# Two transformer stacks in one kernel: every joint between sites in a new order of input chunks, updates and weight splits

## The chip, the cores and the metric

The kernel runs on one core of a Trainium2 chip. The metric is the device time of one execution in microseconds, lower is better. TensorE multiplies 128x128 blocks into eight PSUM banks (`B[0]` to `B[7]`), VectorE (DVE), ScalarE (ACT) and GpSimd (POOL) work on tiles, SyncE (SP) issues most loads. Each engine runs its own instructions in order; semaphores tie them together.

## What is computed

The first block is two layers of latent attention, convolution, Fourier and gating branches on 256 tokens of width 1024. The second block, where the change sits, is twice this, for `x` of 256 x 1024:

```
h = rmsnorm(x, g[0]); x = x + 0.5 * rmsnorm(swiglu(h, w_gate0, w_up0, w_down0), g[1])
h = rmsnorm(x, g[2]); x = x + rmsnorm(token_mixer(h, w_in, w_out, ...), g[3])
h = rmsnorm(x, g[4]); x = x + 0.5 * rmsnorm(swiglu(h, w_gate1, w_up1, w_down1), g[5])
swiglu(h, g, u, d) = (silu(h @ g) * (h @ u)) @ d          # inner width 2816
rmsnorm(x, g) = x * rsqrt(mean(x * x) + 1e-6) * g
```

All in fp32 precision: each product is made of three products of a high and a low part.

## The kernel before

**Sites.** The second block is six sites (`SITES`): feed-forward 0, mixer 0, feed-forward 1, feed-forward 2, mixer 1, feed-forward 3. This text calls the stretch before site i joint i: joint 0 follows the first block, joints 1 and 4 lead from a feed-forward site into a mixer, joints 2 and 5 from a mixer into a feed-forward site, joint 3 from feed-forward 1 into feed-forward 2.

**Weights.** SyncE fills a ring of three 1 MB slots (`fill`, L525; `ffn`, L548). A slot holds two units of 128 x 1024. In a feed-forward site the slots come as gate, up, down; the units as gate half 0, up half 0, gate half 1, up half 1, down, and so on: unit 5 is the first of the second gate slot. For every unit ScalarE copies a high part (`high`, L987) and VectorE subtracts it to get the low part (`low`, L1570). There are six places for split units (`SPLIT`), so a high part waits until TensorE has used the unit six before (`s_used`). A slot is filled again when the low part of its last unit is done (`s_low`), so the second gate load of a site waits for the third unit's low part. `EARLY = 4`: up to four units of the next site are split ahead.

**A joint.** Each engine does `site_tail(i)` and then `site_norm(i + 1)`.
- The sums y of the site stand in banks 4 to 7, one per (token tile t, half hf of 512 columns). ScalarE squares each (L1051), takes the mean's parts (L1054) and the root (L1057).
- VectorE multiplies y by the gain (`gained`, L1634), takes the reciprocal (L1639) and updates the residual `X` with two passes of 512 columns a tile (`update`, L1644). Its order: gain both halves and update for tile 0, then the same for tile 1.
- TensorE warms up with a few products into bank 0 (`warm`, L2438) and transposes the eight 128-column chunks of each tile (`turned`, L2447): chunks 0 to 3 of tile 0, a warming product of 512, chunks 4 to 7 of tile 0, then all eight of tile 1.
- ScalarE copies each turned chunk (L1032) as the high input, VectorE makes the low input (`site_norm`, L1608). Chunks 6 and 7 share banks with 4 and 5 and wait for their low inputs.
- TensorE runs `first_units` (L2467): for each chunk four products of high inputs with high and low weights of two units (L2474, L2475), then two per chunk with low inputs (L2479).
- For the norm, ScalarE squares `X` (`x_square`, L994), VectorE sums and makes a diagonal (`inverse`, L1612), TensorE spreads it over the partitions (`norm_sum`, L2459) and ScalarE copies the row (`norm_row`, L1041). In a feed-forward site `norm_sum` stands after chunk 3 of the third unit, in a mixer right after `first_units`.
- The mixer's first results are scaled by that row when evicted (`evicted`, L1744). In a feed-forward site the row scales the gate (`gate_scaled`, L1658), then ScalarE's Silu (L1066), the product (`multiplied`, L1670), ScalarE's `hidden_high` (L1072) and VectorE's `hidden_low` (L1679), which the first down product waits for (`down`, L2519).

**The last down rows** of a feed-forward site (L2556 to L2564) run the first of three units over all four (t, hf), and then, for each (t, hf), the other two. VectorE and ScalarE split the last two down units and three units of the next site behind and between the last hidden parts (L1108 to L1119, L1725 to L1739), and the fourth in `site_norm`.

**Joint 0.** The last results of the first block are scaled into `ytmp` and added to the residual (`out_scaled`, L1271), the additions of three of the four (t, hf) on GpSimd (L671; those in `ADDED` on VectorE). Then squares (L1008), a root (L1016) and `final_scaled` (L1575), one tile after the other, with low parts of units 0, 2 and 1 between.

## Time and profile before

| | |
|---|---|
| median of 3 runs | 1435.17 us (1432.9 to 1436.27) |
| profiled execution | 1436.06 us |
| its span | 1434.1 us |
| TensorE busy | 1398.1 us |
| VectorE busy | 1018.7 us |
| ScalarE busy | 726.7 us |
| GpSimd busy | 86.7 us |

The profile is one execution, times in microseconds from the span's start. The execution's own time is the span and about 2 us around it. A busy TensorE can be a TensorE that warms up or runs at half clock, so joints are read from the order of instructions.

### The profile page before, as it was taken

To read this page: it belongs to the slowest core of one execution; us is meant where nothing else is said; L and a number is where in the kernel's file an instruction comes from. 1 tells how busy PE (TensorE), PEld (TensorE's weight loads), DVE (VectorE), ACT (ScalarE), POOL (GpSimd) and SP (SyncE) were. 2 spreads that over 40 slices of the span, in tenths; PEclk is the share of its full clock that TensorE was granted. 3 is DMA by queue.
4 is the path that set the end of the run, shared out by engine and by line. 5 is a ranking of instruction groups with operands and counts; after the bars stand their busy time and mean duration, and the time that the engine had idled before them with its cause. 6 is when DMAs were issued, how large, how long until landed. Compare 5 with 4: busy or idle time off the path is not lost.

```text
span 1434.1 us, 22170 instructions
## 1 busy us (share of the span) xinstructions
PE 1398.1 (97%) x8053; PEld 1159.8 (81%) x8053; DVE 1018.7 (71%) x1693; ACT 726.7 (51%) x1244; POOL 86.7 (6%) x103
## 2 busy tenths in 40 slices
PE   5999999999999999999999999999999999999998
PEld 2778747869768888888888888888888888888887
DVE  2588454469677777787686777877777876877776
ACT  3433264345565444475664444654445756644444
POOL 0301211220110000000200000000000002000000
PEclk9999999999999999999999999999999999999999
DMA  9622184275235655754345556646655643455662
GB/s 354 195 88 89 59 285 175 88 221 150 88 133 170 198 189 175 248 176 146 118 133 176 175 193 193 211 153 202 197 183 177 195 142 118 133 176 178 202 196 98
DMA packets 185654, 243.03 MB, mean 169 GB/s; under 512 B 4560, under 2 KB 154608, under 8 KB 185456
## 3 DMA queue, kind: packets, MB, share of 16 engines
q1 hardware_dynamic: 182272, 229.43, 49.9%
q0 software_dynamic: 2736, 10.55, 2.2%
q10 hardware_dynamic: 576, 2.10, 0.4%
q8 instruction: 46, 0.75, 0.2%
q14 instruction: 24, 0.20, 0.0%
HBM read 241.01 MB, written 1.05 MB: 169 GB/s over the span
## 4 chain that ended last, share of the span: by engine, by line
PE 69%; DVE 12%; DMA 9%; ACT 5%; issue 4%; POOL 0%; SPq 0%; DVEq 0%; ACTq 0%; POOLq 0%
PE bank L1977 33%; PE bank L2496 13%; PE bank L2498 7%; DMA weight_ring<-in_w_ffn_up 5%; DVE weights_low L1573 3%; ACT weights_high L992 3%; DVE arena L1567 2%; PE bank L2104 2%; DMA weight_ring<-in_w_ada 2%; DMA weight_ring<-in_w_ffn_down 2%; PE bank L1958 1%; DMA weight_ring<-in_w_in 1%; PE bank L2324 1%; PE bank L2474 1%; PE bank L2475 1%
## 5 line engine op out<-in xcount | busy, mean ns | idle before, releaser
L1573 DVE TENSOR_TENSOR weights_low<-weight_ring,weights_high 128x1024 fp32r<-128x1024 f32 x328 | 393.3, 1223 | 128.8 <-ACT weights_high L992 128.7
L992 ACT ACTIVATE weights_high<-weight_ring 128x1024 fp32r<-128x1024 f32 x328 | 334.6, 1048 | 102.1 <-PE bank L1977 62.0
L2496 PE MATMUL bank<-input_split,weights_high 128*128 128x512 f32 x1280 | 319.5, 391 | 0.0
L2496 PEld LDWEIGHTS bank<-input_split,weights_high 128*128 128x128 f32 x1280 | 234.7, 188 | 45.0
L2498 PEld LDWEIGHTS bank<-input_split,weights_low 128*128 128x128 f32 x1280 | 174.6, 190 | 12.5
L2498 PE MATMUL bank<-input_split,weights_low 128*128 128x256 f32 x1280 | 178.5, 282 | 0.0
L1977 PE MATMUL bank<-weights_high,hidden_high 128*128 128x512 f32 x352 | 138.8, 394 | 1.2 <-DVE hidden_low L1682 1.2
L1066 ACT ACTIVATE silu_gate<-gate_sum 128x256 f32<-128x256 f32 x88 | 36.7, 418 | 202.0 <-DVE gate_sum L1660 200.5
L1977 PE MATMUL bank<-weights_low,hidden_high 128*128 128x512 f32 x352 | 137.9, 392 | 0.0
L1977 PE MATMUL bank<-weights_high,hidden_low 128*128 128x512 f32 x352 | 137.0, 389 | 0.0
L1977 PE MATMUL bank<-input_split,weights_high 128*128 128x256 f32 x576 | 105.6, 285 | 0.0
L1072 ACT ACTIVATE hidden_high<-hidden 128x256 fp32r<-128x256 f32 x88 | 36.8, 418 | 129.8 <-DVE hidden L1673 123.7
L1977 PE MATMUL bank<-weights_high,input_split 128*128 128x256 f32 (+1 forms) x384 | 90.2, 323 | 0.5 <-issue 0.5
L1977 PEld LDWEIGHTS bank<-input_split,weights_high 128*128 128x128 f32 x576 | 89.5, 192 | 1.1 <-DVE qk_feature_major L1756 0.7
L1977 PE MATMUL bank<-hT_high,first_high 128*128 128x512 f32 (+1 forms) x248 | 89.6, 361 | 0.2 <-DVE weight_ring_low L1253 0.2
L1977 PE MATMUL bank<-hT_high,weight_ring_low 128*128 128x512 f32 (+1 forms) x248 | 86.9, 350 | 0.0
L1977 PE MATMUL bank<-input_split,weights_low 128*128 128x256 f32 x288 | 81.4, 283 | 0.0
L1977 PEld LDWEIGHTS bank<-weights_high,hidden_high 128*128 128x128 f32 x352 | 66.4, 189 | 14.3 <-issue 2.8
L1977 PEld LDWEIGHTS bank<-weights_high,hidden_low 128*128 128x128 f32 x352 | 66.1, 188 | 14.5
L1977 PEld LDWEIGHTS bank<-weights_low,hidden_high 128*128 128x128 f32 x352 | 66.4, 189 | 10.7
L1977 PEld LDWEIGHTS bank<-weights_high,input_split 128*128 128x128 f32 x384 | 64.4, 190 | 8.6 <-issue 3.5
L1682 DVE TENSOR_TENSOR hidden_low<-hidden,hidden_high 128x256 fp32r<-128x256 f32 x88 | 37.4, 425 | 43.7 <-ACT hidden_high L1072 43.7
(358 smaller groups left out, 2267.5 us busy)
## 6 DMA issues: line engine op xcount, KB each, us to landing
weight_ring<-in_w_ffn_gate SPq DMA_DIRECT2D x44, 1024.0 KB, 5.3
weight_ring<-in_w_ffn_up SPq DMA_DIRECT2D x44, 1024.0 KB, 5.3
weight_ring<-in_w_ffn_down SPq DMA_DIRECT2D x44, 1024.0 KB, 4.9
weight_ring<-in_w_in SPq DMA_DIRECT2D x32, 1024.0 KB, 5.3
weight_ring<-in_w_ada SPq DMA_DIRECT2D x24, 1024.0 KB, 6.0
weight_ring<-in_w_out SPq DMA_DIRECT2D x16, 1024.0 KB, 5.0
weight_ring<-in_w_in SPq DMA_DIRECT2D x24, 512.0 KB, 4.8
gain_row<-in_norm_gains POOLq DMA_DIRECT2D x6, 512.0 KB, 4.1
```

The lines of the kernel that those rows point to most:

```text
L992: A(unit_in(WH, U), unit_source(U), ACT.Copy).then_inc(s_high, 1)
L1066: A(sgate[:, par, :], gsum[:, par, :], ACT.Silu).then_inc(s_silu, 1)
L1072: A(HBH[:, par if to is None else to, :], hbuf[:, par, :], ACT.Copy).then_inc(s_hh, 1)
L1567: STT(accv, src, w, accv, ALU.mult, ALU.add).then_inc(*done("conv_tap", L, j, k))
L1573: TTn(unit_in(WL, U), unit_source(U), unit_in(WH, U).bitcast(F32), ALU.subtract).then_inc(s_low, 1)
L1682: TTn(HBL[:, to, :], hbuf[:, par, :], HBH[:, to, :].bitcast(F32), ALU.subtract).then_inc(s_hl, 1)
L1958: last = mm(b[32 * k:32 * k + 32, :], CS[:, 4 * q + k, :], quarters(n)[:, k, :], start=(q == 0), stop=(q == 1), skip_group_check=True)
L1977: last = mm(o, lhs(x), rhs(y), start=start and m == 0, stop=stop and m == 2, skip_group_check=True)
L2104: last = mm(b[out_rows, 0:ncol], lhs(k), hT[:, k, 0:ncol], start=(k == 0), stop=(k == KD - 1))
L2324: mm(b[:, 0:keys], Q[0:QK, h, seg * T + qt * P:seg * T + (qt + 1) * P], K[0:QK, h, k0:k0 + keys], start=True, stop=True).then_inc(*done("s ...
L2496: mm(b[:, :].rearrange("p (h n) -> p h n", h=2), unit_in(WH, U)[:, k, :], HX[:, k, :, :], start=(k == 0), stop=False, skip_group_check=True)
L2498: last = mm(b[:, 0:T], unit_in(WL, U)[:, k, :], HH[:, k, :], start=False, stop=(k == KD - 1), skip_group_check=True)
```

## The change

What it does, in all engines' queues:
- **Transposes.** Before `first_units` only chunks 0 to 3 of both tiles are turned, with a warming product of 256 between. The other eight transposes run inside `first_units`, behind chunk 2 of the high inputs.
- **Updates.** Tile 1's first 512 columns are updated in two pieces of 256, and its second gain pass stands behind them. `final_scaled` in joint 0 goes by pieces too: tile 0 first half, tile 1 two pieces, then both second halves.
- **Squares.** ScalarE takes the squares of `X` at other places; that of one (t, hf) per joint moves to VectorE (`tensor_tensor_reduce`), but not in joints 2 and 5.
- **Splits.** Behind a feed-forward site, units 2 and 3 of the next site get their high parts in the tail, behind each tile's root, and their low parts behind input chunk 5 and at the end of `inverse`. The last down unit is split before the last hidden parts. In joint 0 the low parts of units 1 and 3 stand behind chunks 3 and 5.
- **Head of a feed-forward site.** High parts of units 4 and 5 stand before the norm row's copy; the low part of unit 4 stands before the first gate sum, that of unit 5 before `hidden_low`. The norm sum moves from before chunk 3 to before chunk 5 of the third unit, in mixers from before that unit to before its chunk 4. Feed-forward 0 starts with units 0 and 2, both gates, then units 1 and 3, with the norm sum before chunk 2 of unit 3.
- **Last down rows.** Tile 0: units one and two, both halves, then unit three; tile 1: all three for half 0, then for half 1.
- **Joint 0.** All additions but one go to VectorE; ScalarE's table load stands behind two high parts.
- Some marks get other names.

The diff, cut to its core:

```diff
-ADDED = [{(0, 1), (1, 1)}, {(1, 1)}]
+ADDED = [{(0, 1), (1, 1)}, {(0, 1), (1, 0), (1, 1)}]
@@ ScalarE
-            A(stat[:, 60:61], eps[:, 0:1], ACT.Sqrt)
             act.wait_ge(*at("attn", 1, 0, 1))
             for unit in (0, 2):
                 high(unit)
+            A(stat[:, 60:61], eps[:, 0:1], ACT.Sqrt)
...
             def site_norm(i):
+                after_ffn = i and SITES[i - 1][0] == "ffn"
+                if i and not after_ffn:
                     x_square(i, 0, 0)
-                    x_square(i, 0, 1)
-                if i and SITES[i - 1][0] == "ffn":
-                    high(unit_base[i] + EARLY - 1)
                 for c in range(KD):
+                    if c == 4:
+                        x_square(i, 1, 0) if i else high(3)
...
-                for hf in range(2):
-                    x_square(i, 1, hf)
+                if not after_ffn:
+                    x_square(i, 0, 1)
+                if i == 0:
+                    x_square(i, 1, 0)
+                x_square(i, 1, 1)
+                if SITES[i][0] == "ffn":
+                    high(unit_base[i] + 4)
                 act.wait_ge(*at("x_mean", "ready", i))
                 A(stat[:, 8:10], stat[:, 6:8], ACT.Sqrt).then_inc(...)
-                high(unit_base[i] + 4)
                 if SITES[i][0] == "ffn":
                     A(stat[:, 60:61], eps[:, 0:1], ACT.Silu)
+                    high(unit_base[i] + 5)
+                else:
+                    high(unit_base[i] + 4)
                 act.wait_ge(*at("norm_sum", i))
                 A(norm_row, B[4][:, 0:T], ACT.Copy).then_inc(*done("norm_row", i))
-                high(unit_base[i] + 5)
+                if SITES[i][0] == "mix":
+                    high(unit_base[i] + 5)
@@ ScalarE, site_tail; the high part stands behind each root
+                            if t and i < 5 and SITES[i][0] == "ffn":
+                                x_square(i + 1, 0, 0)
...
+                    if i < 5 and SITES[i][0] == "ffn":
+                        high(unit_base[i + 1] + EARLY - 2 + t)
@@ ScalarE, end of ffn
                 high(a + 5)
+                high(a + 6)
                 hidden_high(1, f + 2, None, to=2)
-                high(a + 6)
-                for U in ahead[1:]:
+                for U in ahead[1:2]:
                     high(U)
@@ VectorE, site_norm, and the end of inverse
+                    if i == 0 and c == 3:
+                        low(1)
+                    if i == 0 and c == 5:
+                        low(3)
+                    if i and c == 5 and SITES[i - 1][0] == "ffn":
+                        low(unit_base[i] + EARLY - 2)
...
+                if i and SITES[i - 1][0] == "ffn":
+                    low(unit_base[i] + EARLY - 1)
@@ VectorE, site_tail
+                gained(0, 0)
+                gained(0, 1)
+                scale(0)
+                update(0, 0, slice(0, 512))
+                update(0, 1, slice(512, 1024))
+                gained(1, 0)
+                if i == 5:
+                    gained(1, 1)
+                    scale(1)
+                    update(1, 0, slice(0, 512))
+                else:
+                    if SITES[i][0] == "ffn":
+                        dve.wait_ge(*at("x_new", i, 0, 1))
+                        dve.tensor_tensor_reduce(out=XN2[:, 0, 512:1024], in0=X[:, 0, 512:1024], in1=X[:, 0, 512:1024], ...)
+                    scale(1)
+                    update(1, 0, slice(0, 256), "first")
+                    update(1, 0, slice(256, 512))
+                    gained(1, 1)
+                update(1, 1, slice(512, 1024))
@@ VectorE, head of ffn
                 inverse(i)
+                low(a + 4)
                 gate_parts(0, a + 1)
-                up_parts(0, a + 2)
-                low(a + 4)
                 dve.wait_ge(*at("norm_row", i))
                 gate_scaled(0, f0 + 1)
+                up_parts(0, a + 2 if n else 3)
+                multiplied(0, f0 + 1)
                 low(a + 5)
-                multiplied(0, f0 + 1)
                 hidden_low(0, f0 + 1)
@@ TensorE, site_norm
                 turned(0, (0, 1, 2, 3))
-                warm(1)
-                turned(0, (4, 5, 6, 7))
-                turned(1, (0, 1, 2, 3, 4, 6, 5, 7))
+                warm(1, 256)
+                turned(1, (0, 1, 2, 3))
+                return lambda: (turned(0, (4, 6)), turned(1, (4, 6)), turned(0, (5, 7)), turned(1, (5, 7)))
@@ TensorE, first_units
+                step_to = 1 if i else 2
...
+                    if c == 2:
+                        rest_turned()
@@ TensorE, end of ffn
-                down(1, a + 4, f, False)
-                for t in range(2):
-                    for hf in range(2):
-                        for par in range(2):
-...
+                lasts = ((1, a + 4, f), (0, a + 5, f + 1), (2, a + 6, f + 2))
+                for rest in (lasts[:2], lasts[2:]):
+                    for hf in range(2):
+                        for par, U, ready in rest:
+...
+                            down_row(par, U, 0, False, U == a + 6, (hf,))
+                for hf in range(2):
+                    for par, U, ready in lasts:
+                        last = down_row(par, U, 1, False, U == a + 6, (hf,))
```

## Rows read from the trace of the kernel before

**Rows 1.** The page, costliest groups: the two splitting helpers.

```profile
L1573 DVE TENSOR_TENSOR weights_low<-weight_ring,weights_high 128x1024 fp32r<-128x1024 f32 x328 | 393.3, 1223 | 128.8 <-ACT weights_high L992 128.7
...
L992 ACT ACTIVATE weights_high<-weight_ring 128x1024 fp32r<-128x1024 f32 x328 | 334.6, 1048 | 102.1 <-PE bank L1977 62.0
```

**Rows 2.** Windows: length; busy us of PE, PEld, DVE, ACT, POOL; clock; DMA; GB/s.

```profile
417.00:438.50 21.50, 18.95 (x109) 15.65 (x108) 18.08 (x33) 16.72 (x38) 3.10 (x3) 0.92 0.50 172
...
611.30:624.10 12.80, 10.60 (x72) 8.36 (x71) 11.18 (x32) 10.40 (x29) 0.53 (x1) 1.00 0.39 127
...
927.30:943.20 15.90, 15.69 (x105) 13.44 (x103) 14.07 (x30) 13.79 (x30) 0.53 (x1) 1.00 0.47 151
...
1240.70:1256.10 15.40, 15.40 (x105) 13.42 (x104) 13.03 (x28) 13.19 (x29) 0.59 (x1) 1.00 0.26 86
...
422.20:424.20 2.00, 0.00 (x0) 0.00 (x0) 1.91 (x4) 1.86 (x4) 0.00 (x0) 1.00 0.00 0
...
425.70:427.80 2.10, 2.10 (x11) 2.10 (x10) 1.88 (x5) 1.47 (x5) 0.04 (x1) 0.50 1.07 379
...
943.00:1091.00 148.00, 148.00 (x784) 127.64 (x783) 108.55 (x144) 65.91 (x89) 0.00 (x0) 1.00 0.60 192
```

**Rows 3.** Timeline of joint 3, VectorE: start, duration, instruction, idle before.

```profile
928.07 1.28 DVE L1634 TENSOR_TENSOR x_scaled<-bank,gain_row 128x512 f32<-128x512 f32 x2
...
929.46 1.41 DVE L1644 SCALAR_TENSOR_TENSOR residual<-x_scaled,stat,residual 128x512 f32<-128x512 f32 x2
...
942.55 0.43 DVE L1682 TENSOR_TENSOR hidden_low<-hidden,hidden_high 128x256 fp32r<-128x256 f32 x1 [0.89 <-ACT hidden_high L1072]
```

**Rows 4.** Timeline of joint 3, ScalarE.

```profile
928.22 0.29 ACT L1057 ACTIVATE stat<-stat 128x1 f32<-128x1 f32 x1
...
930.63 2.30 ACT L1032 ACTIVATE input_split<-bank,vectors_T 128x256 fp32r<-128x256 f32 x6
...
938.75 0.37 ACT L1041 ACTIVATE scaled_out<-bank 128x256 f32<-128x256 f32 x1
```

**Rows 5.** Timeline of joint 3, TensorE.

```profile
930.27 1.32 PE L2447 MATMUL bank<-const_base,residual 128*128 128x128 f32 x8 [0.21 <-DVE residual L1644]
...
931.34 0.36 PE L2474 MATMUL bank<-input_split,weights_high 128*128 128x256 f32 x1
...
935.26 2.08 PE L2479 MATMUL bank<-input_split,weights_high 128*128 128x256 f32 x16
...
943.23 0.47 PE L1977 MATMUL bank<-weights_high,hidden_high 128*128 128x512 f32 x1
```

**Rows 6.** Timeline of SyncE in joint 3, and the gate loads' time to landing.

```profile
924.74 0.38 SPq L564 DMA_DIRECT2D weight_ring<-in_w_ffn_gate  x1
...
DMA to landing us min/median/max: 5.2/5.3/6.6
```

**Rows 7.** Timeline of joint 1, ScalarE, TensorE and VectorE.

```profile
607.90 1.06 ACT L992 ACTIVATE weights_high<-weight_ring 128x1024 fp32r<-128x1024 f32 x1 [1.97 <-DMA weight_ring<-in_w_in]
...
613.68 0.64 PE L2447 MATMUL bank<-const_base,residual 128*128 128x128 f32 x4 [1.38 <-DVE residual L1644]
...
624.86 0.76 DVE L1756 SCALAR_TENSOR_TENSOR qk_feature_major<-bank,scaled_out 128x256 f32<-128x256 f32 x2 [1.28 <-ACT scaled_out L1041]
...
630.19 0.42 DVE L1756 SCALAR_TENSOR_TENSOR qk_feature_major<-bank,scaled_out 128x256 f32<-128x256 f32 x1 [0.60 <-PE bank L1977]
```

**Rows 8.** Timeline of joint 0, ScalarE, VectorE and TensorE.

```profile
412.44 2.00 ACT L992 ACTIVATE weights_high<-weight_ring 128x1024 fp32r<-128x1024 f32 x2
...
418.69 2.04 DVE L1582 SCALAR_TENSOR_TENSOR residual<-residual,stat,gain_row 128x512 f32<-128x512 f32 x2
...
424.26 1.82 PE L2447 MATMUL bank<-const_base,residual 128*128 128x128 f32 x8 [2.07 <-DVE residual L1582]
```

**Rows 9.** Timeline behind joint 4, VectorE's evictions in the second mixer.

```profile
1126.32 0.76 DVE L1756 SCALAR_TENSOR_TENSOR qk_feature_major<-bank,scaled_out 128x256 f32<-128x256 f32 x2 [1.28 <-ACT scaled_out L1041]
...
1131.65 0.42 DVE L1756 SCALAR_TENSOR_TENSOR qk_feature_major<-bank,scaled_out 128x256 f32<-128x256 f32 x1 [0.85 <-PE bank L1977]
```

More of the change, by code:

```diff
@@ L1538, in layer @@
                 if L:
-                    for b in range(2):
-                        third_branch_low(b)
+                    third_branch_low(0)
+                    third_branch_low(1)
+                    low(0)
+                    out_scaled(1, 0, 0)
+                    low(2)
+                    out_scaled(1, 0, 1)
+                    out_scaled(1, 1, 0)
+                    out_scaled(1, 1, 1)
+                    return
                 for t in range(nt):
@@ L1614, in inverse @@
                     for hf in range(2):
-                        dve.wait_ge(*at("sum_squares", "site", i, t, hf))
+                        if (t, hf) == ((0, 1) if i else (0, 0)) and (i == 0 or SITES[i - 1][0] == "ffn"):
+                            dve.wait_ge(*at("x_mean", "first tile", i))
+                        else:
+                            dve.wait_ge(*at("sum_squares", "site", i, t, hf))
                 TTn(stat[:, 6:8], stat[:, 0:4:2], stat[:, 1:4:2], ALU.add).then_inc(*done("x_mean", "sum", i))
@@ L1734, in ffn @@
                 TTn(hbuf[:, 1, :], B[3][:, 0:T], sgate[:, 1, :], ALU.mult).then_inc(s_h, 1)
-                low(a + 5)
+                low(a + 6)
                 hidden_low(1, f + 2, to=2)
-                low(a + 6)
-                for U in ahead[1:]:
+                for U in ahead[1:2]:
                     low(U)
@@ L2435, in site_norm, with warm @@
             def site_norm(i):
[L2436 removed]
+                def warm(count, width=512):
                     for _ in range(count):
[L2438 removed]
+                        mm(B[0][:, 0:width], ident, KB[:, 0:width], start=True, stop=True)
                 def turned(t, chunks):
@@ L2493, in wide_product @@
                 for k in range(KD):
-                    if site is not None and k == 3:
+                    if site is not None and k == (5 if site else 2):
                         norm_sum(site)
@@ L2526, in ffn @@
                 a = unit_base[i]
-                for r in hand_over(0) + hand_over(1):
+                second = 1 if n else 2
+                for r in hand_over(0) + hand_over(second):
                     pe.wait_ge(*at(*r))
@@ L2693, in mix @@
                         pe.wait_ge(*at(*r))
-                first_units(i, u0, [B[PB2[key]] for key in firsts], 0)
-                norm_sum(i)
-                products(2, 4)
+                first_units(i, u0, [B[PB2[key]] for key in firsts], 0, rest_turned)
+                product(*PROJ2[2], i)
+                products(3, 4)
                 scores(0)
```

137 lines of the change are left out of this document (64 added, 73 removed).

## The prediction

> **What bounds the kernel now.** I read the page first: beside the products, the costliest groups are the two that split a weight unit, the low part on VectorE (1.22 us) and the high part on ScalarE (1.05 us) [rows 1]. Then the windows [rows 2]: inside a feed-forward site TensorE is busy for 148.0 of 148.0 us, so nothing outside the joints (from one site's last product to the next site's first down product) can change much. "Busy" hides the joints, because warming products and a slow clock count as busy. So the joints were read instruction by instruction: their length is 21.5 us into the first feed-forward site (joint 0), 12.8 to the end of the norm sum into the first mixer (joint 1), 15.9 between the second and third feed-forward sites (joint 3), 15.4 after a mixer (joints 2 and 5) [rows 2]. Two rows stand out: a 2.0 us hole in joint 0 after which the granted clock is 0.50, the 1.2 GHz level, for 2.1 us of products [rows 2]; and in joint 1 a high part that sat 1.97 us on a load while the tail's squares were queued behind it [rows 7].
>
> **The sum is made against the profiled execution,** 1436.06 us with a span of 1434.1; that is 0.9 above the median of 1435.17. A measurement of this kernel tells about 0.2% (2.9 us) from no change.
>
> **Joint 3, the pattern.** The root of the last square ends at 928.51 [rows 4], but VectorE was in two gain passes (1.28) and took the reciprocal late; its updates began at 929.46 [rows 3]. The change puts one gain pass behind the update and cuts the update in two. Reciprocal at 928.6, a 256-wide piece (0.43, as the hidden low of that width [rows 3]) from 928.8 to 929.2, first transposes of tile 1 at 929.3 in place of 930.27 [rows 5]. ScalarE's first chunk copy followed its transpose by 0.36 (930.27 to 930.63) and takes 0.38 (2.30 over 6) [rows 4, 5], so the first weight product can go at 930.13; before it waited for all transposes, to 931.34. Gain 1.2. But eight transposes now run inside the products, and they cost what they took, 930.27 to 931.34 for eight, at most 1.07, I take 0.9 without the start-up [rows 5]. The first units (48 products at 0.12, from 2.08 over 16) thus end 0.3 sooner, at 936.9 [rows 5]. The down product came 6.0 after that end, so TensorE wants it at 942.9 in place of 943.23.
>
> **What it is late for.** The third and fourth units' low parts leave the tail: the third now stands behind input chunk 5. That low part frees the ring slot for the next gate load, which was issued at 924.74 [rows 6]. Now VectorE has: update pieces to 929.6, gain 0.64 and update 0.71 to 930.9, four input lows of 0.41 to 932.5, two more that wait for the late transposes (930.13, three chunks of 4 products, half of the 0.9, a copy) to 933.5, then the low part, 934.7. A gate load lands 5.3 after its issue [rows 6]: 940.1. In the new order ScalarE's high part of unit 5, which reads that slot, stands ahead of the norm row's copy. So 1.05 more, and the copy (0.37) ends at 941.5, where it ended at 939.1 [rows 4]. Queued behind it: gate scaling 0.42, Silu 0.42, the product 0.42, and now also a low part of 1.22 ahead of the hidden low of 0.43 [rows 1, 3]; with VectorE's sum of the up bank (0.68) filling part of the Silu, the hidden low ends at 944.6. Before, it ended 942.98, a quarter us ahead of its use [rows 3, 5]. **Joint 3: 1.4 slower.** Bounds: -0.3 (the load does not hold the chain) to +2.2 (both 1.22 and 1.05 come in full on top).
> [...]
>
> **Joint 0.** The first high part started at 412.44 [rows 8], behind a table load of 1.28 and a dummy that now stand after it, so its unit is ready at about 412.2. From there VectorE must do two low parts of 1.22 and seven 512-wide passes of 0.69: 419.5. A square, root and reciprocal take 1.2 more, then a first piece: transposes of tile 1 at 421.2, where they were at 424.26 after a 2.07 us wait [rows 8]. The first product goes at 422.2, not 425.7, and the clock has no 2 us hole to fall in: ten products at 0.21 (2.10 us, 11 records) become 0.12, 0.9 back [rows 2]. Against it 0.9 for the late transposes and 0.9 because a low part now stands before input low 4, on which chunk 6's bank waits. The first units end at 429.7 and not 432.4. The norm sum then stands at chunk 2 of the fourth unit (433.3), only 2.3 before the down product; norm row, scaling, Silu, product, low part and hidden low take 3.6, so TensorE waits 1.3. Down product 436.9, not 438.5. **1.65 faster;** bounds 0.8 (VectorE's passes stretch as beside GpSimd, 1.0 each in the scaling row of [rows 8], alone 0.71 [rows 3]) to 2.8.
>
> **Joint 1.** Moving the third high part behind the first root takes the 1.97 us wait, and the table load behind it, off the squares [rows 7]. The same distance as in joint 3 (last product to end of first units 9.55) gives 620.9 for 623.4. The norm sum now stands four chunks (1.4) into the next unit, so the first eviction is at 623.25 for 624.86 [rows 7]: 1.6. VectorE leads the mixer's first stretch, and one of its waits, 0.60 for TensorE before the fourth eviction, also goes: **2.2 faster**, though TensorE itself would be 2.5 ahead. Bounds 0.8 to 3.1.
> **Joint 4.** No load waited there. First eviction by the same count 1127.15, before 1126.32, 0.85 later; its 0.85 wait before the fourth eviction takes it up [rows 9]: **0**, bounds -0.5 to +0.5.
> **Joints 2 and 5.** All four units are split before the joint, so no load moves. First product 0.75 sooner, late transposes 0.9: 0.1 slower each; the hidden low fits by 0.2. **+0.2**, bounds -0.6 to +1.2 (both slips of a low part partly uncovered).
>
> **At nothing.** The new order of the last down rows gives tile 0 its sums 6 products sooner at the same end. It needs the low part of the second down row after 3 products instead of 12; VectorE has it within 0.1, and would cost 0.1 to 0.4 per site if not. The square moved to VectorE (512 wide) has no row of its shape; the nearest, a 512-wide pass, is 0.64 to 0.69 [rows 3], the 256-wide one 0.42. I take 0.7, which fits before the root is ready; at 1.0 three joints lose 0.3 each. The end of the program: gain and update of the last tile end where they did. GpSimd's gain load moves by 0.5 and nobody waits. The renamed marks cost nothing.
>
> **Sum:** -1.65 -2.2 +0.2 +1.4 +0 = -2.25. On the median: 1432.9.
>
> **Rivals.**
> *A, the late load is covered* (the slot is freed sooner, or the chain has room): joint 3 gives -0.3, total about -4.0, 1431.2. For it: VectorE idles near 928, and ScalarE's table load can overlap the load. Against: both queues are in order.
> *B, the mixer and the transposes eat the starts:* joint 1 leaves 0.8 as VectorE arrives late at every hand-over, total -0.8, 1434.4. For it: TensorE already waited there on evictions.
> *C, the clock falls in every joint (slower).* Eight transposes now stand among the first products and the warming product is halved. In the trace a wait of 1.38 us left the clock of joint 1 at 1.00 [rows 2, 7], the one of 2.07 in joint 0 did not [rows 2, 8]. If the joints crossed between these, each of five would run ten products at 0.21 (+0.9) and eight transposes in 1.82 for 1.32 (+0.5) [rows 5, 8]: 7.0, total +4.8, 1440.0.
> The Trainium skill, TensorE: Matmul & The Clock Gate, section on transpose, says that transposes do not count as busy for the clock, which speaks for this rival; joint 3 in the trace, sixteen transposes between few warming products and a clock of 1.00 [rows 2], does not bear it out.
> *D, the hidden low is late at all four feed-forward sites:* low part ahead of it, norm row behind a high part. It decides when the chain is over 0.25 longer than now; price 1.0 more in joints 2, 5 and 0: total +0.8, 1436.0.
> *E, nothing but joint 0 counts:* the new order moves starts, not ends; this lies within B.
>
> **How the numbers follow.** Forecast 0.50 (own range 1431.4 to 1434.3; 0.18 of it beyond 0.2% faster), A 0.25, B 0.14, C 0.06, D 0.05. Faster: 0.18 + 0.22 = 0.40; slower: C with 0.01 each of B and D, 0.08; the rest, 0.52, within 0.2%. The range 1429.8 to 1436.0 reaches over A's better half (joints 0 and 1 at their bounds) and over D, and leaves out C.
>
> **What would show it.** Right: in joint 0 no granted clock under 1.00 and the first product near 422; in joint 1 no high part waiting on a load before the squares; in joint 3 a high part waiting on the gate load near 940 and a TensorE wait of 1 to 2 us before the first down product; the late transposes after chunk 2. Wrong: a gate load issued before 930 in joint 3 (A); products at 0.21 in any joint (C); TensorE waits before the first down product in joints 2 and 5 (D).

## The result and the profile after

The changed kernel takes 1439.13 us (median of 12 executions) beside 1434.91 for the kernel before (12 executions): ratio 1.0032, interval 1.0023 to 1.0041. It is slower by 0.3%, and 3 us above the end of my range. One of the twelve executions of the changed kernel took 4105.52 us and is left out of the ratio; the other eleven lie between 1435.11 and 1443.81. The profiled execution of the changed kernel took 1439.07 us, with a span of 1437.1.

Both traces were cut at the same two marks in every joint: the first warming product (it follows the last product of the site at once, so it starts the joint), and the first down product or, in a mixer, the first product of the scores. What lies behind this mark is the site's body. Lengths in us:

| stretch | before | after | difference | forecast |
|---|---|---|---|---|
| up to joint 0 | 417.00 | 415.12 | -1.88 | 0 |
| joint 0 | 21.55 | 20.04 | -1.51 | -1.65 |
| feed-forward 0 | 172.73 | 171.85 | -0.88 | |
| joint 1 | 18.81 | 16.00 | -2.81 | -2.2 |
| mixer 0 | 109.08 | 112.60 | **+3.52** | 0 |
| joint 2 | 15.48 | 15.75 | +0.27 | +0.1 |
| feed-forward 1 | 172.65 | 172.72 | +0.07 | 0 |
| joint 3 | 15.93 | 17.79 | +1.86 | +1.4 |
| feed-forward 2 | 171.99 | 172.60 | +0.61 | 0 |
| joint 4 | 16.33 | 16.00 | -0.33 | 0 |
| mixer 1 | 109.11 | 112.37 | **+3.26** | 0 |
| joint 5 | 15.48 | 15.74 | +0.26 | +0.1 |
| feed-forward 3 and end | 177.96 | 178.52 | +0.56 | 0 |

The differences add up to 3.00, that of the two spans. The first row can't be put down to the change: in the first profile of the kernel before, the granted clock is 0.91 between 20 and 40 us, in the other one it is 1.00, and the same stretch varies from 414.9 to 418.4 over the profiles of the kernels below, which share its code there. The joints together come to -2.26, where the prediction said -2.25. **The loss is in the two mixers, 6.78 us, which the prediction had at nothing.** A joint and its mixer are best read together, as part of the loss is a start that was made sooner and then waited away: joint 1 with mixer 0 went from 127.89 to 128.60 us, joint 4 with mixer 1 from 125.44 to 128.37.

The splitting helpers cost what they did [rows 1], in the page's costliest groups:

```profile
L1576 DVE TENSOR_TENSOR weights_low<-weight_ring,weights_high 128x1024 fp32r<-128x1024 f32 x328 | 393.2, 1222 | 128.5 <-ACT weights_high L992 128.5
...
L992 ACT ACTIVATE weights_high<-weight_ring 128x1024 fp32r<-128x1024 f32 x328 | 334.1, 1048 | 103.6 <-PE bank L2013 60.4
```

Windows of the changed kernel (columns as in [rows 2]): joint 0, joint 1 to the start of its norm sum, joints 3 and 5, then in mixer 0 a wait and the stretch behind it, and the like stretch of mixer 1:

```profile
415.12:435.16 20.04, 17.57 (x109) 14.25 (x108) 17.55 (x37) 16.08 (x36) 0.58 (x1) 1.00 0.55 184
...
607.01:618.16 11.15, 10.90 (x81) 9.57 (x80) 9.69 (x30) 7.70 (x18) 0.53 (x1) 1.00 0.27 92
...
924.08:941.87 17.79, 15.67 (x105) 13.47 (x104) 14.51 (x31) 12.62 (x26) 0.53 (x1) 1.00 0.47 147
...
1242.84:1258.58 15.74, 15.49 (x105) 13.48 (x104) 13.34 (x29) 13.08 (x29) 0.59 (x1) 1.00 0.26 82
...
630.70:632.80 2.10, 0.07 (x1) 0.02 (x1) 2.10 (x4) 1.27 (x3) 0.00 (x0) 1.00 0.21 59
...
632.80:636.50 3.70, 3.69 (x18) 3.05 (x19) 3.03 (x13) 1.51 (x7) 0.00 (x0) 0.54 0.82 243
...
1141.20:1145.00 3.80, 3.80 (x21) 3.80 (x21) 3.11 (x16) 1.86 (x8) 0.00 (x0) 0.55 0.81 270
```

No joint has a clock under 1.00 any more; in joint 0 it was 0.50 in a window of 2.1 us before [rows 2]. But in the mixers TensorE now stands still for 2 us, and behind that the clock is at 0.54 and 0.55, so at its lower level of 1.2 GHz for nearly all of 3.7 and 3.8 us.

TensorE's timeline of the changed kernel: joint 0's first product and first down product, the scores product of the second pair of heads in mixer 0, the second down pair of feed-forward 1, joint 3's first down product, the same scores product in mixer 1, and the second down pair of feed-forward 3, each with the wait before it:

```profile
420.30 0.36 PE L2512 MATMUL bank<-input_split,weights_high 128*128 128x256 f32 x1 [0.19 <-ACT input_split L1027]
...
435.16 0.47 PE L2013 MATMUL bank<-weights_high,hidden_high 128*128 128x512 f32 x1 [1.33 <-DVE hidden_low L1718]
...
632.81 0.68 PE L2659 MATMUL bank<-qk_feature_major 64*128 64x128 f32 x4 [2.04 <-DVE qk_feature_major L1792]
...
777.11 0.49 PE L2013 MATMUL bank<-weights_high,hidden_high 128*128 128x512 f32 x1 [0.67 <-DVE hidden_low L1718]
...
941.87 0.47 PE L2013 MATMUL bank<-weights_high,hidden_high 128*128 128x512 f32 x1 [1.88 <-DVE hidden_low L1718]
...
1140.10 0.49 PE L2659 MATMUL bank<-qk_feature_major 64*128 64x128 f32 x4 [2.04 <-DVE qk_feature_major L1792]
...
1284.45 0.49 PE L2013 MATMUL bank<-weights_high,hidden_high 128*128 128x512 f32 x1 [0.79 <-DVE hidden_low L1718]
```

In joint 0 the 2.07 us wait of [rows 8] is gone, and 1.33 stand before the down product instead, as forecast. The largest waits are 2.04 us in each mixer and 1.88 in joint 3.

**The mixer, followed back.** The scores product at 1140.10 waits for an eviction (a copy out of a PSUM bank) by VectorE. This is what VectorE, ScalarE and SyncE did before (changed kernel, mixer 1, timelines of the three engines):

```profile
1139.58 0.74 DVE L1792 SCALAR_TENSOR_TENSOR qk_feature_major<-bank,scaled_out 128x256 f32<-128x256 f32 x2
...
1137.31 2.35 DVE L1576 TENSOR_TENSOR weights_low<-weight_ring,weights_high 128x1024 fp32r<-128x1024 f32 x2
...
1135.76 0.17 DVE L1805 RECIPROCAL stat<-stat 128x2 f32<-128x2 f32 x1 [2.02 <-ACT score_maps L1139]
...
1134.74 0.40 ACT L1139 ACTIVATE score_maps<-score_maps,stat 128x128 f32<-128x128 f32 x1
...
1133.45 1.28 ACT L1139 ACT_TABLE_LOAD   x1
...
1131.42 2.01 ACT L992 ACTIVATE weights_high<-weight_ring 128x1024 fp32r<-128x1024 f32 x2 [1.93 <-DMA weight_ring<-in_w_in]
...
1125.38 1.53 SPq L532 DMA_DIRECT2D weight_ring<-in_w_in  x2
...
1124.14 1.22 DVE L1576 TENSOR_TENSOR weights_low<-weight_ring,weights_high 128x1024 fp32r<-128x1024 f32 x1
```

Read upward from the last line: the fourth unit's low part ends at 1125.36 and frees its ring slot; the load of units 8 and 9 goes out at 1125.38; ScalarE's high part of unit 8 waits 1.93 us for it, until 1131.42; the exponentials stand behind the two high parts and a table load; VectorE's reciprocal waits 2.02 for the exponentials; then come 2.35 us of low parts, and then the eviction. The same chain in the kernel before:

```profile
1122.53 1.22 DVE L1573 TENSOR_TENSOR weights_low<-weight_ring,weights_high 128x1024 fp32r<-128x1024 f32 x1
...
1123.77 6.67 SPq L532 DMA_DIRECT2D weight_ring<-in_w_in  x4
...
1129.48 1.06 ACT L992 ACTIVATE weights_high<-weight_ring 128x1024 fp32r<-128x1024 f32 x1 [0.35 <-DMA weight_ring<-in_w_in]
...
1138.92 0.75 DVE L1756 SCALAR_TENSOR_TENSOR qk_feature_major<-bank,scaled_out 128x256 f32<-128x256 f32 x2
```

From the start of the joint the load was issued at 8.55 before and at 10.91 now; the high part waited 0.35 and now 1.93; the eviction began at 23.70 and now at 25.11. TensorE wants it at 23.6 (23.9 before). What holds the load is the fourth unit's low part, in both kernels. The change put it behind the whole of `inverse`.

Mixer 0 is another case. There the load goes out at 11.36 where it went out at 10.59, and the eviction begins even sooner than before, at 25.28 and not at 26.16; but joint 1 is 2.8 us shorter, and TensorE wants it at 23.76, where it was 26.34. So in mixer 0 most of the wait is a gain of joint 1 that isn't kept, in mixer 1 it is a chain that got later.

Joint 3, timelines of SyncE, ScalarE and VectorE in the changed kernel, which answer to [rows 3, 4, 6]:

```profile
931.95 0.38 SPq L564 DMA_DIRECT2D weight_ring<-in_w_ffn_gate  x1
...
937.30 1.06 ACT L992 ACTIVATE weights_high<-weight_ring 128x1024 fp32r<-128x1024 f32 x1 [2.67 <-DMA weight_ring<-in_w_ffn_gate]
...
938.27 0.36 ACT L1043 ACTIVATE scaled_out<-bank 128x256 f32<-128x256 f32 x1
...
941.20 0.42 DVE L1718 TENSOR_TENSOR hidden_low<-hidden,hidden_high 128x256 fp32r<-128x256 f32 x1
```

This is the mechanism the prediction described: gate load late (7.9 us into the joint; in the kernel before it went out 2.6 ahead of it), a high part waits 2.67 us for it, the norm row's copy stands behind it, and the hidden low part ends late.

### The profile page after: what moved, and what is told of

Its sections match the earlier page's. It is cut to its first block, busy times and chain, and to the rows that moved or that the text cites. A ratio compares the mean times of both kernels' runs of the same rounds, so it can differ in the third digit from the quotient of the medians.

```text
span 1437.1 us, 22163 instructions
## 1 busy us (share of the span) xinstructions
PE 1397.0 (97%) x8053; PEld 1160.8 (81%) x8053; DVE 1023.0 (71%) x1709; ACT 725.3 (50%) x1236; POOL 83.3 (6%) x101
## 4 chain that ended last, share of the span: by engine, by line
PE 78%; DVE 10%; DMA 5%; ACT 4%; issue 3%; SPq 0%; POOL 0%; DVEq 0%; ACTq 0%; POOLq 0%
PE bank L2013 38%; PE bank L2538 17%; PE bank L2540 9%; DVE arena L1570 2%; PE bank L2140 2%; DVE weights_low L1576 2%; DMA weight_ring<-in_w_ffn_up 2%; DMA weight_ring<-in_w_ada 2%; DMA weight_ring<-in_w_in 1%; PE bank L1994 1%; ACT weights_high L992 1%; PE bank L2360 1%; PE bank L2385 1%; DVE weight_ring_low L1256 1%; PE bank L2711 1%
```

## The experiments

Each is the changed kernel with the edit shown, unless said otherwise. Ratios are to the kernel before on the same chip, in the same set of runs. The medians of the kernel before on the chips used are 1431.83 (first four runs), 1432.32 (next four) and 1434.93 (last four), so times and ratios of different sets are compared with care.

**Theory L:** the fourth unit's late low part makes the mixer's load late, and with it the exponentials, evictions and scores. **Rivals:** VectorE's own order holds TensorE, which merely comes sooner (V); the norm sum takes over the wait (S).

```diff
@@ VectorE, end of site_norm
+                if SITES[i][0] == "mix":
+                    low(unit_base[i] + EARLY - 1)
@@ VectorE, end of inverse
-                if i and SITES[i - 1][0] == "ffn":
+                if i and SITES[i - 1][0] == "ffn" and SITES[i][0] == "ffn":
                     low(unit_base[i] + EARLY - 1)
```

> The changed kernel with one step put back, in the two mixers alone: the fourth unit's low part stands before the norm's sums again and not behind the diagonal. It frees the ring slot of the loads on which ScalarE's ninth high part waits 1.92 and 1.93 us in the changed kernel. Theory L (this late low part makes the mixer's load late, the exponentials behind it late, and TensorE's wait of 2.04 us for the second pair's scores): the slot's load is issued about 1.2 us sooner, TensorE's wait falls from 2.04 to under 1 us in both mixers, and the clock stays at 1.00 behind it; 1.0 to 2.0 us of waiting and about 1.8 us of half clock less per mixer, 4 to 7 us in all: 1432 to 1435. Rival V (TensorE merely comes sooner and VectorE's own order of work holds it): the wait stays near 2 us and the time at 1438 to 1439. Rival S (the norm sum now waits for the diagonal instead): a new wait of up to 1 us before the norm sum, and half of the gain is lost.

Measured: 1433.25 us, ratio 1.0007 [0.9998, 1.0016]. Mixers 109.87 and 109.35 us. Timelines of SyncE, ScalarE and TensorE in its mixer 1:

```profile
1122.30 9.57 SPq L532 DMA_DIRECT2D weight_ring<-in_w_in  x6
...
1127.99 2.01 ACT L992 ACTIVATE weights_high<-weight_ring 128x1024 fp32r<-128x1024 f32 x2 [0.29 <-DMA weight_ring<-in_w_in]
...
1136.79 0.49 PE L2661 MATMUL bank<-qk_feature_major 64*128 64x128 f32 x4 [0.58 <-DVE qk_feature_major L1794]
```

The load goes out 9.61 us into the joint (10.91 before this edit), the high part waits 0.29, TensorE 0.58. In mixer 1 L holds: all four profiles that leave this chain as it is have a wait of 2.04 there. In mixer 0 the wait fell only to 1.10, though no high part waits for a load any more: the norm sum comes 0.4 later there, the small part of S that is true, and ScalarE's exponentials now wait 0.72 for VectorE, which is V. And 1.10 shows less of L than it seems to: the changed kernel itself, run again, had 1.09 in that place (below).

**The same wait, taken from its other end,** with the loads left as they are:

```diff
@@ VectorE, mix
-                low(u0 + 8)
-                low(u0 + 9)
                 evicted(4)
                 evicted(5)
+                low(u0 + 8)
+                low(u0 + 9)
```

> The changed kernel with VectorE's two evictions for the second pair of scores ahead of the low parts of units 8 and 9 (2.35 us) in both mixers; loads untouched. Theory L and rival V both give a shorter wait for the scores (2.04 to about 0), so this prices the wait and the clock behind it: L and V say 2 us of waiting and 1.8 us of half clock less per mixer, less up to 0.5 that the low part of unit 8 is then late: 5 to 7 us in all, 1432 to 1434. The ninth high part still waits about 1.9 us on its load. If instead the exponentials, not the evictions, hold TensorE, a new wait of 1 to 2 us appears at the products of unit 8 and the gain is under 2 us.

Measured: 1432.59, ratio 1.0003 [0.9994, 1.0012]; mixers 109.52 and 110.22. No wait for the scores; a new one of 1 us further on, of which I had expected half. TensorE and ScalarE in mixer 1:

```profile
1144.62 0.65 PE L2684 MATMUL bank<-weights_T,v_token_major 128*64 128x256 f32 x4 [1.01 <-issue]
...
1129.33 2.01 ACT L992 ACTIVATE weights_high<-weight_ring 128x1024 fp32r<-128x1024 f32 x2 [2.53 <-DMA weight_ring<-in_w_in]
```

The high part still waits 2.53 us on its load. So the load's lateness costs little by itself (the mixers are 0.4 and 1.1 us longer than before); most of its price comes through what is queued behind it on two engines.

**What is the clock's share?** Idle products in TensorE's wait:

```diff
@@ TensorE, scores(p), ahead of the wait for qk_ready
+                    if p == 1:
+                        for _ in range(9):
+                            mm(B[0][:, :], ident, KB[:, 0:512], start=True, stop=True)
```

(The wait for qk_ready moved behind that for the score banks, with the products between.)

> The changed kernel with nine idle products of 512 columns (0.23 us each, 2.07 in all) into a bank that is free, on TensorE just where it waits 2.04 us for the second pair's scores in both mixers. They fill the wait and shorten nothing. If the fall of the clock behind the wait costs by itself, the clock stays at 1.00 and the time falls by 1.5 to 2 us per mixer, 3 to 4 in all: 1435 to 1436. If the clock's fall is covered by other waits, the time stays at 1439.

Measured: 1445.75, ratio 1.0095 [1.0081, 1.0110], mixers 116.50 and 116.49, clock 1.00. A miss, of my own making: I had one such product at 0.23 us. A run with four was meant to mend it, and its text had a product at half of what it takes:

> As the earlier run with warming products in the mixers' wait, but four of them: there nine took about 0.43 us each and so 3.9 us, longer than the wait of 2.04. Four take 1.7 us and fit. If the fall of the clock behind the wait costs by itself, both mixers take about 110.8 us (as the one mixer did whose clock stayed up with the same wait) and not 112.5, and the time is 2.5 to 3.5 us under the changed kernel's, with a small scatter between executions. If not, the mixers stay at 112.5.

Measured: 1437.66, ratio 1.0034 [1.0022, 1.0045], mixers 112.24 and 112.23, clock 1.00. The first row is its timeline, the second that of the next run, with two:

```profile
631.31 3.60 PE L2657 MATMUL bank<-const_base 128*128 128x512 f32 x8
```

```profile
630.85 1.88 PE L2657 MATMUL bank<-const_base 128*128 128x512 f32 x4
```

A product is two records of 0.43 each: 0.86 us. Four take 3.45, outlast the wait by 1.4, and this ate what they kept of the clock.

> The warming run a third time, with two idle products: four took 3.45 us (each product of 512 columns in full precision is two records of 0.43), two take 1.7 and fit into the wait of 2.04. Theory C (the clock's fall behind the wait costs by itself, some 1.5 us each time it happens, and the scatter of the changed kernel is whether it does): no execution has a mean clock under 0.999, both mixers take 109.9 to 111.2 us, the executions scatter by less than 2.5 us, and the ratio to before is 1.0010 to 1.0020 in place of 1.0026 to 1.0032. Rival: the mixers stay at 112.3 or the scatter stays.

Measured: 1437.05, ratio 1.0011 [1.0002, 1.0019], mixers 110.65 and 111.60 (111.2 at most was expected), mean clocks 0.998 to 1.000 (0.999 at least), scatter 3.25 us (2.5). The ratio was 1.0026 and 1.0032 without them, but in other sets of runs, the 1.0026 on another chip, and the 1437.05 itself is no less than the 1436.12 below; so the ratios alone don't show theory C. The mixers do, one against the other inside the profiles: both stand under the 112.4 to 112.6 of those with a fall.

**The changed kernel again:**

> The changed kernel as it is, beside the three others on the same chip. Ratio to before 1.0025 to 1.0040, executions scattered over 4 us or more; each execution with a lower mean clock is longer, by about 1.8 us for every mixer in which the clock fell; those with a mean clock of 0.999 or more lie within 1.5 us of the kernel before.

Measured: 1436.12, ratio 1.0026 [1.0016, 1.0036]. Of its ten executions the four with a mean clock of 0.999 took 1434.55 to 1435.80, the two with 0.998 1435.06 and 1436.43, the four with 0.997 or less 1437.38 to 1438.85. The last clause was wrong: with the clock up, it is still 2.2 to 3.5 us above the 1432.32 of the kernel before. Its profile is one without a fall in the mixers. TensorE in both mixers, and a window of mixer 1:

```profile
633.02 0.49 PE L2659 MATMUL bank<-qk_feature_major 64*128 64x128 f32 x4 [1.09 <-DVE qk_feature_major L1792]
...
1138.10 0.49 PE L2659 MATMUL bank<-qk_feature_major 64*128 64x128 f32 x4 [2.04 <-DVE qk_feature_major L1792]
```

```profile
1136.00:1142.00 6.00, 3.96 (x34) 3.60 (x34) 5.34 (x17) 3.12 (x11) 0.00 (x0) 1.00 0.51 172
```

Here the load landed sooner in mixer 0 (5.4 us after its issue, 6.8 in the first profile), so the wait was 1.09 and the mixer took 109.87. In mixer 1 the wait was the full 2.04, but the clock stayed at 1.00 and the mixer took 111.12. In all the profiles that leave these waits as they are there are seven of 2.04 us. Three kept the clock and their mixers took 110.85, 111.09 and 111.12; three were followed by one fall and took 112.37, 112.46 and 112.60; the seventh is in the next run. So a fall costs about 1.5 us (112.5 against 111.0), and the wait 1.9 (111.0 against 109.1). That the wait is 2.04 each time, though the high part waits anywhere between 1.7 and 2.5 us for its load, is no sign against L. TensorE's last work before the wait, the transposes of the second head's score map, and the eviction both follow one VectorE instruction (it ends 22.93 us into joint 4, the transposes start at 23.07, the eviction comes behind the 2.35 us of low parts). What the load is later than that holds the transposes too.

**Joint 3, and who pays for a late load:**

```diff
@@ ScalarE, site_norm
                     A(stat[:, 60:61], eps[:, 0:1], ACT.Silu)
-                    high(unit_base[i] + 5)
@@ ScalarE, ffn
                 hidden_high(0, f0 + 1, None)
+                high(a + 5)
                 high(a + 6)
@@ VectorE, ffn
-                low(a + 5)
                 hidden_low(0, f0 + 1)
+                low(a + 5)
```

> The changed kernel with the sixth unit's split taken out of the head chain of the feed-forward sites: its high part stands behind hidden_high and its low part behind hidden_low. My prediction's step for joint 3 (a high part waits on the late gate load with the norm row's copy queued behind it): the wait of 1.88 us before the first down product of joint 3 goes to under 0.3, that of 1.33 in joint 0 falls to about 0.8 (there only the low part of 1.22 ahead of hidden_low is gone, half covered by hidden_high); total 2.0 to 2.6 us faster than the changed kernel. Rival (the hidden product is late by itself, through the norm sum's place): both waits stay within 0.4 of what they are, total within 0.8.

Measured: 1441.08, ratio 1.0055 [1.0040, 1.0070]. Both waits did what was expected (joint 3 15.73 us, the wait gone; joint 0 a wait of 0.77), and the total went the other way. TensorE at the second down pair of feed-forward 0 and 2, and the window behind the latter:

```profile
460.75 0.49 PE L2013 MATMUL bank<-weights_high,hidden_high 128*128 128x512 f32 x1 [1.22 <-DVE hidden_low L1718]
...
966.10 0.57 PE L2013 MATMUL bank<-weights_high,hidden_high 128*128 128x512 f32 x1 [1.88 <-DVE hidden_low L1718]
```

```profile
966.00:972.00 6.00, 5.90 (x19) 4.70 (x20) 4.79 (x7) 2.65 (x5) 0.00 (x0) 0.72 0.96 324
```

The waits moved one pair on: 1.22 in feed-forward 0, and in feed-forward 2 the same 1.88 that joint 3 had, now with a clock of 0.72 behind it. That site takes 175.55 in place of 172.60. Feed-forward 0 and joint 3's site together give back what the joints won: with their joints they take 192.85 and 191.29, against 191.89 and 190.39 in the changed kernel. Mixer 1 takes 114.25 us in this profile. It has the same wait of 2.04, and then

```profile
1140.40:1147.30 6.90, 6.47 (x31) 5.85 (x32) 5.56 (x18) 1.86 (x8) 0.00 (x0) 0.51 0.49 154
```

a clock at its lower level for nearly all of 6.9 us. The edit changes nothing there, so the total of this run tells its worth only roughly. The load was moved instead:

```diff
@@ VectorE, site_norm
-                    if i and c == 5 and SITES[i - 1][0] == "ffn":
+                    if i and c == 5 and SITES[i - 1][0] == "ffn" and not (i - 1 == 2):
@@ VectorE, site_tail, ahead of scale(1)
+                    if i == 2:
+                        low(unit_base[i + 1] + EARLY - 2)
```

> The changed kernel with, in joint 3 alone, the third unit's low part moved from behind input chunk 5 back into the tail, ahead of the reciprocal of tile 1, where VectorE idles 0.70 us. It frees the slot of the gate load, so that load is issued near 925.8 and not at 931.95, and lands near 931. Theory (one late load is paid wherever it is waited for: at the head it cost 1.88 us, with the head's order changed it was paid in the next pair): the high part of the sixth unit no longer waits 2.67 us, joint 3 falls from 17.8 to about 16.3 (the update comes 0.5 later), and the next site does not lengthen (172.6 or less): 1.3 to 2 us faster than the changed kernel. Rival (the head is bound by the norm sum's later place): joint 3 stays above 17.2.

Measured: 1436.83, ratio 1.0036 [1.0022, 1.0050]. SyncE, ScalarE and TensorE (the last is the second down pair of feed-forward 2):

```profile
926.64 0.38 SPq L564 DMA_DIRECT2D weight_ring<-in_w_ffn_gate  x1
...
935.30 1.04 ACT L992 ACTIVATE weights_high<-weight_ring 128x1024 fp32r<-128x1024 f32 x1
...
966.96 0.49 PE L2015 MATMUL bank<-weights_high,hidden_high 128*128 128x512 f32 x1 [1.03 <-DVE hidden_low L1720]
```

The load goes out 1.9 us into the joint, the high part waits for nothing, and joint 3 takes 16.10 (expected 16.3). But the second pair then waits 1.03, and joint and site together take 189.17, against 190.39 and 189.75 in the two profiles of the changed kernel. Of the 1.4 to 1.7 us won, 0.5 to 0.8 is given back 26 us later, and the total shows none of it (the changed kernel has 1.0026 on the same chip).

**Three edits together** (the fourth low part, the evictions, the gate load):

> The changed kernel with three edits together: the fourth low part ahead of the norm's sums in mixers, the second pair's evictions ahead of the low parts of units 8 and 9, and the third low part of joint 3 in the tail. Mixers near 109.2 each (from 112.5), joint 3 near 16.3 (from 17.8), the rest as in the changed kernel: 7 to 8 us under an execution of it with the clock down, 1.0 to 2.0 us under the kernel before (ratio 0.9985 to 0.9995). Rival (VectorE has no room: what is taken off one wait comes back at the next hand-over of the mixer): mixers at 110, ratio 1.000 or more.

Measured: 1432.75, ratio 0.9999 [0.9991, 1.0008]; mixers 109.38 and 109.35, joint 3 16.08, all as expected, and no gain on the kernel before. TensorE in feed-forward 2:

```profile
967.06 0.49 PE L2017 MATMUL bank<-weights_high,hidden_high 128*128 128x512 f32 x1 [1.79 <-DVE hidden_low L1722]
```

1.79 us of waiting again, with the clock at 0.91 over the 20 us around it: the site takes 175.44. So the rival was right in kind, but for this site and not for the mixers. How much of it the median holds isn't shown: the profiled execution is the slowest of the twelve (1437.14, mean clock 0.996; the others have 0.998 to 1.000).

**Joint 3 back in its old order,** with the two mixer edits; this is the core of the edit (`OLD = {3}`), and the rest of it gives tail, squares, updates and transposes of that joint their old order:

```diff
@@ VectorE and ScalarE, end of ffn
-                for U in ahead[1:2]:
+                for U in ahead[1:(None if i + 1 in OLD else 2)]:
@@ VectorE, end of site_norm
+                if SITES[i][0] == "mix" or i == 3 and i in OLD:
+                    low(unit_base[i] + EARLY - 1)
@@ VectorE, head of ffn
+                if i in OLD:
+                    gate_parts(0, a + 1)
+                    up_parts(0, a + 2)
+                    low(a + 4)
...
```

> The changed kernel with the two mixer edits of before (fourth low part ahead of the norm's sums, second pair's evictions ahead of the low parts of units 8 and 9) and with joint 3 in the order of the kernel before. Joint 3 with the site behind it falls from 189.7 to 190.4 us (changed kernel) to about 187.9 (kernel before), the mixers stand at 109.2 to 109.6; 1.8 to 2.5 us under the run with the two edits but the new joint 3: ratio to before 0.9975 to 0.9992. Rival (the second pair of that site is bound by its loads whatever the joint does): joint 3 and its site take 189 or more.

Measured: **1431.46 us, beside 1434.93 before: ratio 0.9975 [0.9964, 0.9986]**, faster than both kernels. Joint 3 takes 15.77, its site 172.18, together 187.95 (kernel before 187.92); mixers 109.37 and 109.37. The rival falls. Its joint 3 in one window:

```profile
922.52:938.29 15.77, 15.72 (x106) 13.53 (x104) 13.28 (x29) 13.03 (x30) 0.53 (x1) 1.00 0.38 129
```

This is measured on one chip, the one on which the kernel before is slowest; whether the gain is as large on the others isn't shown.

> As the run with joint 3 in the old order, and joints 2 and 5 too; only joints 0, 1 and 4 stay new. My prediction gave the new order 0.1 us of loss in each of joints 2 and 5, the traces 0.26: 0.2 to 0.6 us faster than with joint 3 alone, ratio 0.997 to 0.999. If the new joints 2 and 5 gave something further on, it is slower than that run.

Measured: 1431.74, ratio 0.9974 [0.9965, 0.9983]. Joints 2 and 5 take 15.49 each, 0.26 less than in the new order, but the 0.2 to 0.6 us expected don't show: the whole can't be told from the run with joint 3 alone.

**The kernel before, on the chip of the last runs:**

> The kernel before itself, for a profile on the chip of these runs. If the clock's fall in joint 0 (0.50 for over 2 us in the first profile) comes in every execution, joint 0 takes 21.5 us again; if it comes in some, joint 0 takes about 20.6 here and the changed kernel's gain there is smaller than the first two profiles show.

Measured: 1434.43 us; joint 0 takes 21.73, with the clock down, and joint 1 18.06, where the first profile had 18.81. Window of its joint 0:

```profile
424.00:428.00 4.00, 3.99 (x22) 3.85 (x21) 3.25 (x9) 3.37 (x9) 0.58 (x1) 0.57 1.00 345
```

So joint 0 takes 21.5 to 21.7 us in both profiles of that kernel, and the gain of 1.5 there is real where its clock falls. It doesn't always: of its executions beside the runs, 11 of 23, 6 of 23 and 1 of 31 on the three chips have a mean clock of 1.000, which leaves no room for 3.4 us at 0.50 in 1433 (that would make 0.999). There the gain in joint 0 must be smaller; no profile shows by how much. In joint 1 the gain is 2.06 by this profile and 2.81 by the first.

## Why the prediction was wrong, point by point

**Right: the joints.** Their sum was -2.26 for -2.25; so close a sum is luck, as single joints missed by up to 0.6 and the misses cancel. Joint 0: first product 5.2 us into the joint, as forecast (at 420.30), with the clock at 1.00, and a wait of 1.33 before the down product (1.3 forecast). Joint 1: no high part sits on a load ahead of the squares; against the two profiles of the kernel before it gained 2.81 and 2.06, for a forecast of 2.2. Joint 3: each link as written, 1.86 in place of 1.4, inside its bounds; the gate load went out 0.5 us later than I had worked out (7.9 for 7.4 us into the joint). Joints 2 and 5: 0.26 each for 0.1; the eight late transposes cost their 0.9, but the first product came 0.63 sooner and not 0.75.

**Wrong: the step "Joint 4. No load waited there", and the mixers at nothing with it.** The first paragraph took from one window of a feed-forward site (148.0 of 148.0 us busy) that nothing outside the joints can change much; a mixer had no window. I followed a delayed low part to the slot it frees in one joint only. In joint 3 the third unit frees the gate's slot, and I counted it through to the down product. In joints 1 and 4 the slots hold two neighbours, so it is the fourth unit that frees one, and this one stood even later, behind the diagonal. I priced the mixer by its first four evictions [rows 7, 9] and stopped 7 us short of the eviction that this load decides. There TensorE waits 2.04 us, up from 0.35, in both mixers. In mixer 1 the run with this low part alone put back cuts the wait to 0.58 and the mixer by 3.0 us, of which about 1.5 is the clock's. In mixer 0 it is 2.7 us against the first profile of the changed kernel and nothing against the second (109.87 in both), so there this run shows no share of the load; what fails there as much is the sentence on joint 1 that 2.2 are kept "though TensorE itself would be 2.5 ahead": joint 1 and mixer 0 together are 0.7 us longer in the first profile, and 2.0 shorter in the second, where the wait is 1.09 and the clock stays up (15.99 and 109.87).

**Wrong in place: the clock.** Rival C let it fall in the joints, after transposes, with a chance of 0.06. It fell in the mixers, after a wait, and gave nearly the time of that rival (1440.0) by another way; that the numbers meet is luck. Its price of 1.4 for a fall was right (1.5 measured). My own row said where the danger is: in the trace of before a wait of 2.07 us lost the clock and one of 1.38 did not [rows 2, 7, 8]. I used it for joints and did not ask where new waits of 2 us would come up. As for the Trainium skill, TensorE: Matmul & The Clock Gate, and its section on transpose: no joint of the changed kernel lost its clock with eight transposes among the first products (1.00 in all four windows above); the rule did not bear here.

**Missed, smaller:** the second down pair. Feed-forward 2 is 0.2 to 0.6 us longer behind the new joint 3, and what the runs won in joint 3 with its new order was waited for there again, in part or in full.

The sum, then: joints -2.26; two waits of 1.9; two falls of 1.5 in a profile that has both; 0.4 in the feed-forward sites. That is 4.9, which is what the two traces differ by without their first stretch. The medians differ by 4.2 and the ratio of 1.0032 is 4.6; how many falls a median execution has isn't shown.

## To carry to other kernels

When a splitting or copying step is moved, write down for each site which buffer it frees, which transfer waits for that buffer, and who reads the transfer, and follow this to the reader even where it lies 14 us on, as here from the end of the fourth low part (10.9 into joint 4) to the eviction (25.1); a pattern worked out for one kind of site doesn't hold for the next. A start made sooner is only kept if the weight chain starts sooner too; otherwise the wait reappears one pair later, or in the mixer behind the joint. And a wait near 2 us on TensorE is to be priced with a possible fall of the clock behind it, here 1.5 us in four of seven cases, once twice that.

## What the runs showed of the hardware that I had not expected

The same wait of 2.04 us in the same place was followed by a lower clock in some executions and not in others. With the clock up behind it the mixer took 110.85, 111.09 and 111.12 us, with the fall 112.37, 112.46 and 112.60, and with a fall of twice the length 114.25. Elsewhere a wait of 1.79 and one of 1.88 at a second down pair lost it, while 1.88 and 2.07 at joint 3's down product and 1.82 at joint 0's did not; no wait of 1.09 or 1.10 lost it. This goes with the scatter of the changed kernel, 8.7 us (1435.11 to 1443.81) where the kernel before scatters over 4.6: its executions with a mean clock of 0.999 took 1435.11 and 1436.32, those with 0.996 or less 1441.42 to 1443.81. The Trainium skill, TensorE: Matmul & The Clock Gate, in the section "What's actually happening", says that the gate follows how busy the engine was lately and isn't aligned with the kernel; that the same wait in the same place went both ways agrees with it. Two warming products (1.7 us of work that computes nothing) in the wait were followed by a clock of 1.00 in both mixers of the one profile.

A full-precision product of 512 columns with the identity is two records, 0.86 us (eight records in 3.60 us for four products), not the 0.23 of the split products beside it.

What stays open: why the second down pair of a feed-forward site waits 0.3 to 1.0 us in some executions of both kernels and not in others was not tried. Nor was the full order of the kernel before with the two mixer edits, so how much of the last ratio the new joints 0, 1 and 4 give is read from the traces alone.
